# A two-block transformer kernel on one core: reads of moved squares a slot sooner and loads two pieces later in the sync queue, the first difference scores a slot sooner, the first turn of the values two slots later

## The reference, cut to what matters

```python
# first block, twice
u = rms_norm(x) @ w_in                     # qa ka va za qb kb vb zb ga gb, 1024 columns each
ya = dilated_mixture(rope(qa), rope(ka), va) * silu(za)        # 16 heads of 64
ob = diff_attention(rope(qb), rope(kb), vb, lam)               # 8 heads, two score maps each
yb = rms_norm(ob) * (1 - lam_init) * silu(zb)
x = x + (sigmoid(ga) * (ya @ w_proj_a) + sigmoid(gb) * (yb @ w_proj_b)) @ w_out
# second block, twice
q, k, v = silu(causal_conv(h @ w_in, 4 taps))                  # dn_q, dn_k, dn_v
y_a = gated_delta_rule(q, k, v, g, beta)   # chunks; the inverse of a unit triangular matrix
y_b = swa_sink_attention(...)              # 16 heads, window of 128
x = x + rms_norm((sigmoid(ga) * (y_a @ w_up_dn) + sigmoid(gb) * (y_b @ w_up_sw)) @ w_o)
x = x + rms_norm(relu(h2 @ w_ff1) ** 2 @ w_ff2)
```

## Time and profile before

| | us |
|---|---|
| median of 3 runs (lowest, highest) | 1692.28 (1691.61, 1692.85) |
| the profiled execution's own time | 1694.67 |
| its span, first to last instruction | 1692.9 |
| TensorE busy | 1661.0 |
| VectorE, ScalarE, GpSimd busy | 1178.2, 945.7, 228.1 |
| mean granted TensorE clock, 1 being 2.4 GHz | 0.996 |

### The profile page before, as it was taken

How to read it: one execution, slowest core, us unless ns; L and a number is a source line. 1 busy time by engine, 2 the same in 40 slices (tenths; PEclk the granted TensorE clock), 3 DMA queues, 4 the chain that set the end, 5 groups by cost and what they waited for, 6 DMA issues and landing times.

```text
span 1692.9 us, 29240 instructions
## 1 busy us (share of the span) xinstructions
PE 1661.0 (98%) x11295; PEld 1358.0 (80%) x11295; DVE 1178.2 (70%) x2176; ACT 945.7 (56%) x1786; POOL 228.1 (13%) x318
## 2 busy tenths in 40 slices
PE   9998999999989999999999999999999999999998
PEld 8886788888867788877787788888877787788887
DVE  6768667766776666778877676666678877676665
ACT  5456475544655754578644455456577644554553
POOL 2203000022110000432302000000332302000000
PEclk9999999999999999999999999999999999999999
DMA  8768744558687354633323546554633333445552
GB/s 313 263 208 266 271 131 166 181 202 272 211 277 234 125 199 162 205 120 125 109 95 123 170 156 211 181 180 149 224 125 125 101 100 126 162 162 205 180 180 82
DMA packets 154661, 299.54 MB, mean 177 GB/s; under 512 B 7455, under 2 KB 18843, under 8 KB 153499
## 3 DMA queue, kind: packets, MB, share of 16 engines
q1 hardware_dynamic: 152464, 294.81, 51.8%
q10 hardware_dynamic: 2059, 2.85, 0.5%
HBM read 281.91 MB, written 15.73 MB: 176 GB/s over the span
## 4 chain that ended last, share of the span: by engine, by line
PE 81%; DVE 5%; ACT 5%; issue 3%; POOL 3%; DMA 3%; SPq 0%; DVEq 0%; ACTq 0%; POOLq 0%
PE bank L463 20%; PE bank L465 19%; PE bank L464 19%; PE bank L444 5%; PE bank L446 3%; PE bank L497 2%; DMA scratch<-pair 2%; DVE lo L426 2%; PE bank L455 1%; PE bank L454 1%; PE bank L453 1%; ACT scratch L2069 1%; PE bank L1857 1%; ACT hi L416 1%; DVE buf L2221 1%
## 5 line engine op out<-in xcount | busy, mean ns | idle before, releaser
L463 PE MATMUL bank<-hi,xhl 128*128 128x512 f32 (+1 forms) x1728 | 697.4, 404 | 3.1 <-DVE lo L426 1.5
L465 PE MATMUL bank<-hi,xhl 128*128 128x512 f32 (+1 forms) x1728 | 673.6, 390 | 0.0
L464 PE MATMUL bank<-lo,xhl 128*128 128x512 f32 (+1 forms) x1728 | 672.0, 389 | 0.0
L426 DVE TENSOR_TENSOR lo<-raw,hi 128x1024 fp32r<-128x1024 f32 (+1 forms) x504 | 612.3, 1235 | 57.4 <-PE bank L465 39.6
L416 ACT ACTIVATE hi<-raw 128x1024 fp32r<-128x1024 f32 (+1 forms) x504 | 518.7, 1050 | 192.3 <-PE bank L465 156.1
L463 PEld LDWEIGHTS bank<-hi,xhl 128*128 128x128 f32 x1728 | 325.6, 188 | 83.2 <-issue 16.4
L465 PEld LDWEIGHTS bank<-hi,xhl 128*128 128x128 f32 x1728 | 325.0, 188 | 70.6
L464 PEld LDWEIGHTS bank<-lo,xhl 128*128 128x128 f32 x1728 | 326.2, 189 | 58.5
L444 PE MATMUL bank<-xhl,hi 128*128 128x512 f32 x384 | 136.0, 398 | 0.0
L446 PE MATMUL bank<-xhl,lo 128*128 128x256 f32 x384 | 107.8, 281 | 0.0
L444 PEld LDWEIGHTS bank<-xhl,hi 128*128 128x128 f32 x384 | 72.1, 188 | 17.8
(11 more groups left out here) (321 smaller groups left out, 1919.2 us busy)
## 6 DMA issues: line engine op xcount, KB each, us to landing
raw<-in_w_in SPq DMA_DIRECT2D x135, 1024.0 KB, 5.2
raw<-in_w_ff SPq DMA_DIRECT2D x64, 1024.0 KB, 5.3
raw<-in_w_proj_a SPq DMA_DIRECT2D x8, 1024.0 KB, 5.0
raw<-in_w_proj_b SPq DMA_DIRECT2D x8, 1024.0 KB, 5.0
raw<-in_w_out SPq DMA_DIRECT2D x8, 1024.0 KB, 5.2
raw<-in_w_up_sw SPq DMA_DIRECT2D x8, 1024.0 KB, 5.0
raw<-in_w_up_dn SPq DMA_DIRECT2D x8, 1024.0 KB, 5.1
raw<-in_w_o SPq DMA_DIRECT2D x8, 1024.0 KB, 5.0
```

The costliest lines, as they stand in the source:

```text
L426: dve.tensor_tensor(self.lo[g % LO_RING][:, 0:w], src, self.hi[g % HI_RING][:, 0:w].bitcast(F32), ALU.subtract).then_inc(self.lo_ready, 1)
L463: pe.matmul(out, xh[:, row, t], self.hi[slot % HI_RING][:, w], start=first, stop=False)
L464: pe.matmul(out, xh[:, row, t], self.lo[slot % LO_RING][:, w], start=False, stop=False)
L465: mm = pe.matmul(out, xl[:, row, t], self.hi[slot % HI_RING][:, w], start=False, stop=last)
```

## The change

Four edits:

1. `LOAD_LEAD` 11 to 9: the sync engine's loads stand two pieces later in its order, behind the `lo` of an earlier piece.
2. `a_land` of pair u from slot 2u+5 to slot 2u+4. In slot 2u+5 it stood behind the load of that slot's piece and ahead of `a_move` of pair u+1; now it stands ahead of the load.
3. `b_scores` of head 0 from the slot behind the first piece of `ga1` to the slot behind the last piece of `ga0`. All other steps of the difference attention stay where they were.
4. `turn` of `dv` 0 from slot 1 to slot 3 of `delta_slots`, where it stands behind `betas` 1, `decays` 1 and `square` of `dq`.

```diff
-LOAD_LEAD = 11
+LOAD_LEAD = 9
@@ flipped_values
-                   + ([(f"{kind}_land", t // 2 - 2)] if 5 <= t <= heads + 3 and t % 2 else [])
+                   + ([(f"{kind}_land", t // 2 - 2)] if 4 <= t <= heads + 2 and t % 2 == 0 else [])
@@ plan_one
     work = difference(DHEADS)
-    p.run(sec("ga", 8), [[]] * 4 + work[:4])
-    p.run(sec("gb", 9), [b + a for a, b in zip(work[4:12], [[]] * 8)])
-    p.run(sec("zb", 7), work[12:18] + [[("head_norm",)], []])
+    work = work[:1] + [[]] + work[1:]
+    p.run(sec("ga", 8), [[]] * 3 + work[:5])
+    p.run(sec("gb", 9), work[5:13])
+    p.run(sec("zb", 7), work[13:19] + [[("head_norm",)], []])
@@ delta_slots
-    for at, name, n in ((1, "dv", 0), (9, "dv", 1), (11, "dv", 2), (17, "dv", 3), (21, "kd", 0), (25, "v", 0),
+    for at, name, n in ((3, "dv", 0), (9, "dv", 1), (11, "dv", 2), (17, "dv", 3), (21, "kd", 0), (25, "v", 0),
```

## The result

The changed kernel takes 1704.31 us (median of 5 runs, 1700.78 to 1705.86) against 1692.85 us of the kernel before on the same chip (5 runs, 1691.61 to 1698.21). The ratio is 1.0063, 95% interval 1.0051 to 1.0075: slower by 11.5 us, where +4.5 was forecast, and 1.3 us beyond the end of the range. The direction was right, the size was not. The profiled execution has a span of 1699.0 us and a time of its own of 1700.78, the shortest of the five; that turns out to matter.

What follows compares the result with a forecast made beforehand. TensorE, busy 98% of the span, was taken as the bound. Edits 1 and 2 -7.7, edit 3 +3.0, edit 4 +6.1 and +3.1 for the clock gave +4.5 us on 1692.28: 1696.8 us, range 1685.5 to 1703.

Steps and rivals of the forecast that it cites:

- 7.7 us gained: Edits 1 and 2: products of pair 7 start earlier, at 180.7 and 509.7, gaining 3.0 + 4.7 us.
- rival (a): The forecast itself, 1696.8 us; own range 1693.5 to 1702, circles of 7.8 to 8.5 us; chance 0.42.
- The circle: Sync queue's round of read, load, four writes and wait for the last write, forecast at 8.1 us, bounding the last pairs.
- in waits of 1 to 2 us without a drop of the clock: Sign of being right: `a_out` waits shrink from 10.4 to some 6 or 8 us, spread so over pairs 5 to 7.
- the 4.0 us that slow clock had cost before: TensorE around pairs 5 to 7: the halved clock costs 1.5 us in layer 0 and 2.5 in layer 1.
- Nothing overlaps between the circles: Sync queue after edits 1 and 2: each round is bounded by the landing of its last write.
- all 14.4 us of the first paragraph: What edits 1 and 2 work on: 10.4 us of products' waits for reads plus 4.0 us of slow clock.
- rival (c): Sync-queue circles of 7.4 us, no product waits for a read: -2.2 us, 1690.1; chance 0.15.
- (e): Queue edits gain 0, a strict circle being no faster than the old overlap: +12.2 us, 1704.5; chance 0.10.
- (b): As (a), but the clock stays up behind the turn of `dv` 1 after 3.3 us of wait: 1693.7; chance 0.15.
- (d): Edit 4's convolution costs nothing and the 0.8 us waits at the turn of `dv` 1 go: -6.3, 1686.0; chance 0.13.
- (f): (c) and (d) together: -13.0 us, 1679.3; chance 0.05.

Runs made afterwards that it cites:

- second profile of the changed kernel: The whole change run once more, unchanged, on the chip of other follow-up runs: 1703.16 us (6 runs), ratio 1.0047 to the kernel before.
- lead of 7: LOAD_LEAD taken from 11 to 7 on the kernel before, nothing else: 1679.01 us (4 runs), ratio 0.9920.

## Why the prediction was wrong

**The step that failed is the term for edits 1 and 2, "7.7 us gained"**. By itself that term measures -2.8 us (edits 1 and 2 alone, -3.7 by the ratio), and it missed mainly because the clock was forecast to stay up behind the products' waits and fell there. The other terms held: with the measured -2.8 in place of -7.7 and everything else as forecast, the sum is -2.8 + 3.0 + 6.1 + 3.1 = +9.4, or 1701.7 on 1692.28, inside the range. With the measured 3.1 and 10.0 for edits 3 and 4 it is +10.3, and +9.8 and +11.5 were measured in the two jobs. The bounds were also added up too narrowly: the worst case that rival (a) names itself, circles of 8.5 us and 2.5 us for each drop, comes to -2.1 + 3.0 + 6.1 + 5.0 = +12.0, or 1704.3, and not 1702. That is just the time measured, though by another way, since it was slow clock at pair 7 more than longer circles that took the gain.

Within the term, point by point:
- The circle was sized right for layer 1 and 0.5 us short for layer 0: 8.1 us forecast, 8.0 and 8.6 measured. The last products came at 509.12 for a forecast of 509.7, and at 181.96 for 180.7, so that the 7.0 us of earlier start stand beside 7.7. In layer 0 that is partly luck: seven circles took 3.7 us more than reckoned, but the first read went out at 118.18, 1.7 us sooner than reckoned, and the last landed 0.8 us sooner. In this execution the step held.
- What did not hold is "in waits of 1 to 2 us without a drop of the clock". A product waits for as long as its read lands later than TensorE gets there, 6.50 us after the pair before, and the last pair has the longest waits, 2.98 and 2.10 us: its read went out 9.2 us behind the one before in layer 0 (169.36 to 178.57), and in layer 1 its product started only 4.2 us after its issue, with the read of flipped `qb` issued ahead of it. In the kernel with edits 1 and 2, and in the second profile of the changed kernel, the clock fell behind these waits. The 7.7 held the 4.0 us that slow clock had cost before; 3.0 of them came back at pair 7. In the profile of edits 1 and 2 the last products start 1.6 and 5.3 us sooner, and 3.7 us are left at the first scores of layer 1, which is about the measured size of the term.
- The sum was also carried from the profiled execution to the median without asking what that execution held. Its time was 1694.67, 2.4 us above the median, and it had both drops of the clock. Gains that remove its drops should be worth less to the median; this was argued, not tried. The profile after shows the reverse: 3.5 us below its median, with no drop at pair 7. Profile against profile the difference is +6.1 us, close to the +4.5 forecast, and median against median +11.5.
- "Nothing overlaps between the circles" was right, and it is what makes the term poor. I took the circle of before as a given and did not ask what edit 1 does alone. It frees the load from the late `lo`, so that it goes out right behind the writes, where the queue only waits, and that by itself takes away all 14.4 us of the first paragraph: the gain of rival (c), reached by one half of the edits, while the other half undoes it. The read ahead of the load makes the queue wait first (65.5 us in place of 14.7) and the load then stands 0.5 us ahead of the next writes, which land in 5.4 us in place of 3.1. Shown by the kernels with edit 1, with edit 2 and with both.

**Edit 3.** Forecast 1.5 us a layer at the scores for ScalarE's reading of the banks; measured 1.62, and 3.1 to 4.5 us in time. Right. It brought nothing in return.

**Edit 4.** Forecast 6.1 us of stand, 3.05 in each layer, and 3.1 of clock. In the first layer the turn is 3.12 us later against the sums of squares ahead of it. The wait at the turn of `dv` 1 grew by 5.0 us, and 1.1 of the 1.8 us for the convolution in front of `gb1` are the two long ones of 0.56: 6.1. From the turn to the products of line 1835 (1834 of before) it took 26.53 and 25.42 us in place of 23.8, so the clock cost 2.7 and 1.6 us, 4.3 in place of 3.1. VectorE's idle of some 5 us was measured as 4.96. The reason is shown by the turn in the same slot ahead of the wait: it costs nothing.

**The rivals.** (e), 1704.5 at a chance of 0.10, has the number, in part by luck, since it put the gain at nothing and it was 2.8 us. Its reason, that a strict circle is no faster than the old overlap, is most of the truth: the strict circle with the later load gains 2.8 us, and the same circle with the old lead (edit 2 alone) loses 5.7. The row that spoke for it in the prediction, two reads in 15.2 us of the old order, should have weighed more than 0.10. (b), that the clock stays up behind 3.3 us, is true of some executions and not of others. (c) wanted circles of 7.4 us, and they took 8.0 and 8.6; (d) was ruled out by the 3.3 us at the turn, and (f) with both. The Trainium skill's fit for a transfer of the GpSimd path ("DMA: Bandwidth & Descriptors", the section on the anatomy of one DMA) had given an estimate of 6.2 us for the six transfers of a circle, taken as one. Measured were 8.0 and 8.6 us a circle, so the estimate is too short for a strict circle through this queue, where each round waits for a write and starts with a read.

**A version that beats both kernels**: edit 1 with the turn of `dv` 0 in slot 3 ahead of the betas, 1678.17 us, 14.4 us under the kernel before and 25 to 26 under the changed one (two jobs). Edit 1 alone gives 14 of them; the turn's part, 0.8 us against the lead of 7 in the same job, is what the small waits for ScalarE at the turns lost (1.6 to 0.8 us).

**What stays open.** Why the clock falls behind some waits of 2 to 3.3 us and not behind others of the same length was not settled. And why the read ahead of the load costs the kernel of before 5.7 us but the one with edit 1 11.7 was only argued from the order of the queue, not tried in steps. Nor was it tried why writes right behind a load land later.

## What to carry to other kernels

Where one queue both waits for its own writes and issues loads that nobody needs yet, let the load go out behind the writes and ahead of the read that waits for them, and see that it waits for nothing there: the wait for the writes is then its cover. The right order alone is not enough; the kernel before had it, and its loads stood 29.7 us for a late `lo` in one layer. Issuing the waiting read first looks sooner and makes the round a strict circle. Work that was ahead of an engine's wait stays cheap only ahead of it; here a later slot was harmless, and a place behind the wait cost nearly the full length (3.12 of 3.50 us in the first layer, and the clock besides). And take a change apart before you add it up: here two edits meant for one end were worth -14.4 and +11.7 us.

## What the runs showed of the hardware

- The granted clock fell to 0.50 behind a wait of 3.30 us and stayed at 1.00 behind one of 3.27 us at the same step (edits 1 and 4), and in two profiles of the changed kernel it fell behind 2.63 and 1.94 us and stayed up behind 2.98 and 2.10. One drop cost 1.5 to 2.7 us. The executions of a kernel with such waits lay 4.4 to 11.8 us apart (edits 1 and 4, edit 2 alone), those of the three kernels without any (edit 1, edit 1 with the turn ahead of the wait, lead 7) 0.6 to 1.0 us, and those of edits 1 and 3, with waits of 1.62 us, 2.1.
- The same write lands in 3.1 us in the median when the load went out 2.6 to 6.5 us ahead of it (edit 1), and in 5.4 when it went out 0.5 us ahead (the changed kernel). A read issued as soon as its writes have landed, ahead of the load, lands in 3.0 us; behind the load it takes 5.8 (before) or 5.2 (edit 1).
